# Gate/up products of a mixture-of-experts stage: matmuls of 512 columns in place of pairs of 256

## The reference, cut to what matters

```
def clamped_swiglu(gu):
    gate, up = gu[..., :D_FF_2], gu[..., D_FF_2:]
    gate = jnp.minimum(gate, SWIGLU_LIMIT)
    up = jnp.clip(up, -SWIGLU_LIMIT, SWIGLU_LIMIT)
    return (up + 1.0) * (gate * jax.nn.sigmoid(gate * SWIGLU_ALPHA))
...
    logits = (hf @ router_w + router_b).astype(jnp.float32)
    top_logit, top_idx = lax.top_k(logits, TOP_K)
    gates = jax.nn.softmax(top_logit, axis=-1)
...
    def expert_block(args):
        xb, e = args
        y = clamped_swiglu(xb @ w_gu[e] + b_gu[e])
        return y @ w_down[e] + b_down[e]
```

## Time and profile before

| | |
|---|---|
| median of 3 runs | 3562.39 us (3554.3 to 3566.34) |
| profiled execution, its own time | 3559.63 us |
| its span, first to last instruction | 3557.8 us |
| experts stage within the span | about 2490 to 3523 us |
| mean granted TensorE clock | 0.909 |
| TensorE matmul busy | 2979.3 us, 84% |
| DMA traffic | 683.36 MB |

### The profile page before, as it was taken

The page is one execution under the profiler, slowest core; times in us unless marked ns, Lnnn a source line. Parts: engine busy times, 40 slices in busy tenths (PEclk is TensorE's granted clock), DMA queues, the critical chain, the costliest instruction groups (busy, mean ns, idle before and its releaser), DMA issues. The chain is left out here.

```text
span 3557.8 us, 89384 instructions
## 1 busy us (share of the span) xinstructions
PE 2979.3 (84%) x39874; PEld 2132.5 (60%) x39874; DVE 1400.8 (39%) x2286; ACT 888.9 (25%) x1555; POOL 325.3 (9%) x253
## 2 busy tenths in 40 slices
PE   5978879999787888887897995775989899899895
PEld 3855558888474676675696885544445455454453
DVE  3355553333854554555565675425110111011003
ACT  2114322222222433331344453302100100011001
POOL 0021200000310223231000002202000000000001
PEclk7989799999897999998898997886999899899897
DMA  7242432222134100103554440135899999999996
GB/s 292 84 147 79 169 139 75 95 95 95 55 133 153 45 28 21 51 4 125 190 183 153 146 141 27 47 129 185 342 405 408 401 395 408 393 402 407 395 403 239
DMA packets 194167, 683.36 MB, mean 192 GB/s; under 512 B 24224, under 2 KB 39072, under 8 KB 144624
## 3 DMA queue, kind: packets, MB, share of 16 engines
q1 hardware_dynamic: 174720, 650.86, 47.5%
q10 hardware_dynamic: 17904, 22.28, 1.7%
q0 software_dynamic: 1152, 4.19, 0.3%
HBM read 651.86 MB, written 25.43 MB: 190 GB/s over the span
## 5 line engine op out<-in xcount | busy, mean ns | idle before, releaser
L3574 PE MATMUL experts_psum_gu<-ring,experts_x 128*32 128x256 f32 x7680 | 470.6, 406 | 22.4 <-issue 22.4
L3574 PEld LDWEIGHTS experts_psum_gu<-ring,experts_x 128*32 128x32 f32 x7680 | 247.5, 117 | 234.4 <-issue 76.2
L3692 DVE TENSOR_SCALAR experts_gate<-experts_psum_gu 128x768 f32<-128x768 f32 (+1 forms) x32 | 26.4, 824 | 911.2 <-PE experts_psum_gu L3574 911.2
L3599 PE MATMUL experts_psum_down<-down_weights,experts_hiddenT 128*32 128x256 f32 x5120 | 287.7, 382 | 3.0 <-ACT experts_hiddenT L3642 3.0
L3599 PEld LDWEIGHTS experts_psum_down<-down_weights,experts_hiddenT 128*32 128x32 f32 x5120 | 155.8, 111 | 129.1 <-ACT experts_hiddenT L3642 3.2
L3636 ACT ACTIVATE experts_sigmoid<-experts_gate 128x768 f32<-128x768 f32 (+1 forms) x32 | 23.7, 739 | 660.2 <-DVE experts_gate L3692 660.2
L818 PE MATMUL mlp_psum_bank<-mlp_x_high,mlp_w_high 128*128 128x512 f32 (+1 forms) x512 | 175.5, 343 | 12.3 <-DVE xT_rounded L322 12.3
L296 DVE TENSOR_TENSOR ring_rounded<-ring,mlp_w_high 128x1024 fp32r<-128x1024 f32 x128 | 156.7, 1225 | 50.7 <-ACT mlp_w_high L291 50.7
L818 PE MATMUL mlp_psum_bank<-xT_rounded,mlp_w_high 128*128 128x512 f32 (+1 forms) x512 | 173.7, 339 | 0.0
L818 PE MATMUL mlp_psum_bank<-mlp_x_high,ring_rounded 128*128 128x512 f32 (+1 forms) x512 | 173.2, 338 | 0.0
L1792 POOL TENSOR_TENSOR rwkv_Lo<-rwkv_L,chunk_masks 128x512 f32<-128x512 f32 x80 | 116.6, 1473 | 445.8 <-DVE rwkv_L L2235 340.5
(11 more groups left out here) (759 smaller groups left out, 5838.4 us busy)
## 6 DMA issues: line engine op xcount, KB each, us to landing
ring<-in_w_gu SPq DMA_DIRECT2D x186, 1024.0 KB, 9.8
down_weights<-in_w_down SPq DMA_DIRECT2D x128, 1024.0 KB, 12.2
ring<-in_ada_w SPq DMA_DIRECT2D x36, 2048.0 KB, 8.4
ring<-in_mlp_w SPq DMA_DIRECT2D x32, 2048.0 KB, 7.9
xT<-in_w_gu SPq DMA_DIRECT2D x64, 1024.0 KB, 10.7
ring<-in_w_in SPq DMA_DIRECT2D x12, 2048.0 KB, 7.8
ring<-in_ab_w_in SPq DMA_DIRECT2D x6, 2048.0 KB, 9.8
ring<-in_w_rkv SPq DMA_DIRECT2D x6, 2048.0 KB, 8.4
```

The lines of the kernel that those rows point to most:

```text
L3574: mm = nc.tensor.matmul(pg[32 * j:32 * j + 32, q, gr, :], x, w[:, c:c + C], start=False, stop=(u == U - 1), skip_group_check=True)
L3599: mm = nc.tensor.matmul(pd[32 * c:32 * c + 32, gr, :], hidT[:, a, gr, GROUP * v:GROUP * v + GROUP], w[:, a, C * c:C * c + C], start=(v == ...
L3692: v.tensor_scalar(G, pg[:, 0, 0:groups, :], SWI_LIMIT, None, ALU.min).then_inc(s_gt, 1)
```

## The change

Strip j's gate and up columns are now streamed by one matmul. `strip` makes a view of a unit (or of the bias rows) with two runs of 256 floats, 1024 apart; the result goes to one PSUM bank for each group, gate in its first half and up in its second. The tile `gu` has three banks instead of four. Each bank has its own first matmul, so all bias matmuls start a sum. VectorE reads gate and up from the halves of the banks. Sums, operands and the order of units and groups stay as they are.

```
-        pg = ph.ps("gu", [P, 2, 4, C])
+        pg = ph.ps("gu", [P, GROUPS_A, 2, C])
+        strip = lambda w, j: w.rearrange("p (q j c) -> p q j c", q=2, j=4)[:, :, j, :]
...
                     for gr in range(groups):
-                        for q in range(2):
-                            for j in range(4):
-                                c = 1024 * q + C * j
-                                nc.tensor.matmul(pg[32 * j:32 * j + 32, q, gr, :], who[:, :], b96[:, c:c + C],
-                                                 start=(gr != 1), stop=False, skip_group_check=True)
+                        for j in range(4):
+                            nc.tensor.matmul(pg[32 * j:32 * j + 32, gr, :, :], who[:, :], strip(b96, j),
+                                             start=True, stop=False)
...
                             x = xe[:, u, GROUP * gr:GROUP * gr + GROUP]
-                            for q in range(2):
-                                for j in range(4):
-                                    c = 1024 * q + C * j
-                                    mm = nc.tensor.matmul(pg[32 * j:32 * j + 32, q, gr, :], x, w[:, c:c + C],
-                                                          start=False, stop=(u == U - 1), skip_group_check=True)
+                            for j in range(4):
+                                mm = nc.tensor.matmul(pg[32 * j:32 * j + 32, gr, :, :], x, strip(w, j),
+                                                      start=False, stop=(u == U - 1))
...
-                    v.tensor_scalar(G, pg[:, 0, 0:groups, :], SWI_LIMIT, None, ALU.min).then_inc(s_gt, 1)
-                    v.tensor_scalar(W, pg[:, 1, 0:groups, :], SWI_LIMIT, -SWI_LIMIT, ALU.min, ALU.max).then_inc(s_up, 1)
+                    v.tensor_scalar(G, pg[:, 0:groups, 0, :], SWI_LIMIT, None, ALU.min).then_inc(s_gt, 1)
+                    v.tensor_scalar(W, pg[:, 0:groups, 1, :], SWI_LIMIT, -SWI_LIMIT, ALU.min, ALU.max).then_inc(s_up, 1)
```

## The result

The changed kernel takes 3501.73 us (3501.6 to 3504.75, 4 runs) against 3564.36 us (3554.3 to 3566.42, 4 runs) of the kernel before on the same chip: ratio 0.9832, 95% interval 0.9812 to 0.9852. The span fell by 58.3 us, from 3557.8 to 3499.5.

The account below looks back on a forecast made before the run. TensorE, stopped by late instructions after each jump, was taken as the bound. Its gain of 22.4 + 12 + 3 = 37 us, capped at 34 by the weight stream, less a little, gave 33: 3562.4 to 3529 us, range 3514 to 3562.

Parts of the forecast that it names:

- What bounds the kernel before: Experts loop: TensorE sets the pace, stopped twice per jump by late instructions (62.0 and 22.4 us); DMA has 2 to 3% in hand.
- Columns, bias, VectorE: Gate/up products: no gain from wider matmuls (bounds 0 and 11 us), 3 us from fewer bias matmuls, VectorE's split reads hidden.
- Second stop: Inside a gate/up unit after the jump: longer first instruction supply covers the wait for the next; 22.4 us go.
- Clock: TensorE after the jump: half clock ends sooner, 0.9 us less lost a pass (bounds 0 and 1.9), 12 us over 13 passes.
- First stop: At the experts loop's jump back, ahead of the bias matmuls: 4.4 us a pass, 62.0 in all, stays unchanged.
- rival 3: Experts loop: shorter loop stays held, so the stop at the jump goes too; stream sets pace, 34 to 40 us, 3525; chance 0.08.
- The limit of the stream: Weight loads of the experts stage: at 415 GB/s a pair takes 63.1 us, limiting the gain to 34 us.
- Rival 2: Item B: faster TensorE waits for weights and its clock drops, costing 10 of the 33 us, so 3539; chance 0.10.
- Rivals 1 and 4: 1: stop inside a unit goes, clock no sooner, 3536, chance 0.12. 4: no change but bias term, 3559, chance 0.14.
- Rival 5: Just behind the jump: first instruction supply ends there, TensorE idles until the next; 28 us slower, 3590; chance 0.08.

Follow-up runs that it names:

- pad40: The kernel before with 40 spare bias matmuls ahead of the experts loop, nothing else changed: 3591.56 us, ratio 1.0061 to 1.0127.
- pad46: The kernel before with 46 spare bias matmuls ahead of the experts loop, nothing else changed: 3532.87 us, ratio 0.9914 to 0.9956.
- layout kernel: The changed kernel with its PSUM layout and VectorE reads, but matmuls of 256 columns throughout: 3558.23 us, against 3556.28 of the kernel before.
- item B wide: The changed kernel with matmuls of 512 columns only in item B, 256 in item A: 3525.23 us, ratio 0.9891 to 0.9931 to the kernel before.
- its twin: The changed kernel with 512 columns only in item B, plus 48 spare matmuls ahead of the loop: 3508.45 us, ratio 0.9846 to 0.9879.

## Why the prediction was wrong

**What bounds the kernel before.** Right. The two stops are instructions that have not arrived (pad40 and pad46 move the second at will), and TensorE sets the pace.

**Columns, bias, VectorE.** Right: nothing of note (20.8 for 20.9 us; the layout kernel measures no change). The bias product of item A takes 0.83 where it took 0.84, so the 3 us granted for it were not there.

**Second stop.** Right in mechanism and size. Where it alone goes, the medians fall by 32 us (item B wide), 30 (46 spare matmuls, their 6.6 us taken off) or 25 (55, 7.7 us off), each against the kernel before on its chip; the experts stage in the profiles falls from 1028.2 us by 33, 34 and 30. The forecast was 33. The pairs came out at 60.0 to 64.1 us, most at 61.3 to 63.1, where 62 to 63.5 were named.

**Clock.** The 0.9 us a pass was low. Pairs went from 64.85 to 61.44 us where only the second stop (1.6 us) had gone, which leaves 1.8 for the clock, close to the upper bound of 1.9 of that term.

**First stop.** This is the step that failed: "First stop (4.4 us a pass, 62.0 in all): unchanged, the jump is still there." The jump is, the stop is not: 62.0 us of it before, none after. The change shortens the loop from 2032 to 1352 instructions, from 9 blocks to 6, and up to 7 are kept. I had this as rival 3 and gave it 0.08. My argument against it was that each pass of the kernel before fetches everything anew, 10 packets. That says only that a loop of 9 blocks is not kept; it bears on nothing shorter.

**The limit of the stream.** Mis-sized as well, which is why rival 3 was priced at 3525 and why the range did not reach the result. I took 415 GB/s and left seven instruction packets in each pass. The changed kernel fetches none from the third pass on, and its stream runs at 422. A pair then takes 61.2 us instead of 63.1. How much of the step from 415 or 417 to 422 is the packets' (1.0% of the DMA engines' time) is not shown, since every kernel that fetched also had TensorE stop at the jump.

**How the stage sums up.** From its first to its last matmul it went from 1028.2 us (2492.9 to 3521.0) to 971.5 (2491.0 to 3462.5): 56.6. The first three pairs, in which TensorE lives on the lead, give 23 of them; the next eleven, held by the stream, give 40 (3.6 each); the last pair and the tail take 6.5 back, because the weights now come late there too. The other 2 us of the span lie ahead of the stage and have nothing to do with the change.

**How the gain divides.** From 1028.2 to 995.1 us in the stage with item B alone wide: the second stop and its half clock, 33 us. From there to 971.5: the first stop, its half clock and the instruction packets, 23.6 us. That is far less than the 60 us of stops, and where it comes from shows why. In the first three pairs, on the lead, the changed kernel gains 17 us over that kernel; in the next six, 61.4 us there and 61.2 here, less than 2, since the stream would hold them in any case; in the next five 8, where that kernel has the stop and waits for weights beside it (6.0, 2.9 and 1.5 us in all); the last pair and the tail take 3 back.

**Rivals.** Rival 2 did not happen: TensorE waits eight times a pair, 0.4 to 0.9 us each, and the clock stays at 1.00. The Trainium skill's warning ("TensorE: Matmul & The Clock Gate", HAM oscillation — how this bites in real kernels) is of longer waits than these; the traces agree, with a drop behind every stop of 4 to 5 us at the jump and behind the waits of 3.9 and 2.9 us shown above, and none behind a wait under 1 us. In between it is not the same each time: 3.0 us of idle time late in the kernel with 40 spare matmuls and 3.5 us in the one with 55 left the clock at 1.00. Rivals 1 and 4 were wrong. Rival 5 is real, but not here.

## What to carry to other kernels

A hardware loop on TensorE has a size at which it changes its nature: count its instructions (a float32 matmul is four) and the blocks of 256 that it touches, and keep it within 7. If it can't be, look where its first instruction lies, since with busy DMA engines a short remainder behind the jump target (5 or 85 instructions here) costs a second stop, and a few spare instructions ahead of the loop move it. Then look at what bounds the loop once the stop is gone: here the weight stream took most of what the first stop had cost. When a rival says that a cost goes away altogether, ask whether the evidence against it was taken in the range where the changed kernel will be.

## What the runs showed of the hardware

- TensorE keeps a loop of 6 or 7 blocks of 256 instructions and fetches one of 8 or 9 anew at each pass, mostly with one block more than the loop touches (9 packets of 16 KB for 8 blocks, 10 for 9, and 9 or 10 with 55 spare matmuls).
- A jump to a block that is not there costs 4.1 to 5.5 us with the DMA engines full, 4.05 on average at a share of 0.92. With the engines full the next block comes some 5.5 us after the first; at 0.92 it comes before 25 matmuls are done.
- Instruction packets take 1.0% of the DMA engines' time for 0.6% of the bytes. The weight stream runs at 417 GB/s in the kernel with them and at 422 in its twin without them and without the stop.
- Each stop of 4.1 to 5.5 us at the jump was followed by a TensorE clock of 1.2 GHz. Idle times of 2.9 to 3.5 us were in some runs and not in others; waits under 1 us, eight in 61 us, were not.
- Matmuls of 256 and of 512 columns, four strips side by side, go by at the same rate for each column: 54.4 ns for 256, 108 ns for 512.
